# A hybrid decoder step on one core: chunk products regrouped by kind, part of the scaling moved to ScalarE, two weight splits moved

## What is computed

```python
xc, dtc, bc, cc = r(x), r(dt), r(bm), r(cm)          # r: split in chunks
acs = jnp.cumsum(dtc * a, axis=2)
decay = jnp.exp(jnp.where(causal, seg, -jnp.inf))     # seg: differences of acs
scores = jnp.einsum('bclgn,bcsgn->bclsg', cc, bc)
wgt = scores[..., None] * decay * dtc[:, :, None]
y_diag = jnp.einsum('bclsgk,bcsgkp->bclgkp', wgt, xc)
decay_end = jnp.exp(acs[:, :, -1:] - acs) * dtc
states = jnp.einsum('bclgn,bclgk,bclgkp->bcgkpn', bc, decay_end, xc)
# h is carried from chunk to chunk:  h * chunk_decay + state
y_off = jnp.einsum('bclgn,bcgkpn,bclgk->bclgkp', cc, h_prev, jnp.exp(acs))
y = y_diag + y_off;  y = y + xs * d_skip
```

## Time and profile before

| | us |
|---|---|
| median of 3 runs (lowest to highest) | 2364.67 (2363.91 to 2365.6) |
| the profiled execution | 2363.87 |
| its span, first to last instruction | 2362.2 |
| TensorE busy | 2325.2 (98%) |
| VectorE busy | 1218.1 (52%) |
| ScalarE busy | 593.6 (25%) |
| mean granted TensorE clock | 0.996 |

### The profile page before, as it was taken

The page is one execution under the profiler, slowest core; times in us unless marked ns, Lnnn a source line. Parts: engine busy times, 40 slices in busy tenths (PEclk is TensorE's granted clock), DMA queues, the critical chain, the costliest instruction groups (busy, mean ns, idle before and its releaser), DMA issues.

```text
span 2362.2 us, 37288 instructions
## 1 busy us (share of the span) xinstructions
PE 2325.2 (98%) x15084; PEld 2248.2 (95%) x15084; DVE 1218.1 (52%) x2337; ACT 593.6 (25%) x1020; POOL 58.4 (2%) x100
## 2 busy tenths in 40 slices
PE   8999999999999999999999999999999999999999
PEld 7999999999999999985799988999999999999998
DVE  6544444444445775465867435256444444444445
ACT  6111111111112332235623134141111111111112
POOL 0000000000000000022300000000000000000000
PEclk9999999999999999998999999999999999999999
DMA  4111111111111421057524324311111111111111
GB/s 148 42 48 36 53 36 53 53 49 39 36 53 41 127 58 37 28 171 226 173 81 127 125 97 152 111 54 36 54 36 53 53 52 36 36 52 43 46 36 74
DMA packets 185422, 169.23 MB, mean 72 GB/s; under 512 B 6660, under 2 KB 165138, under 8 KB 185066
## 3 DMA queue, kind: packets, MB, share of 16 engines
q1 hardware_dynamic: 185329, 167.94, 22.9%
HBM read 147.98 MB, written 20.04 MB: 71 GB/s over the span
## 4 chain that ended last, share of the span: by engine, by line
PE 61%; DVE 2%; ACT 1%; issue 0%; DMA 0%; DVEq 0%; ACTq 0%
PE bank L2265 17%; PE bank L2266 17%; PE bank L2267 17%; PE bank L2857 1%; PE bank L2869 1%; PE bank L2753 1%; PE bank L2757 1%; PE bank L2961 1%; PE bank L2889 1%; PE bank L2762 0%; PE bank L2878 0%; DMA w_raw<-in_w_mem_v_dram 0%; PE bank L2911 0%; PE bank L2773 0%; PE bank L2697 0%
## 5 line engine op out<-in xcount | busy, mean ns | idle before, releaser
L2265 PE MATMUL bank<-h_hi,w_hi 128*128 128x352 f32 x3120 | 1011.2, 324 | 5.8 <-DVE h_lo L1351 2.8
L2266 PE MATMUL bank<-h_lo,w_hi 128*128 128x352 f32 x3120 | 1000.6, 321 | 0.0
L2267 PE MATMUL bank<-h_hi,w_lo 128*128 128x352 f32 x3120 | 1000.3, 321 | 0.0
L2265 PEld LDWEIGHTS bank<-h_hi,w_hi 128*128 128x128 f32 x3120 | 586.2, 188 | 7.9 <-DVE w_lo L1322 3.2
L2266 PEld LDWEIGHTS bank<-h_lo,w_hi 128*128 128x128 f32 x3120 | 587.3, 188 | 0.0
L2267 PEld LDWEIGHTS bank<-h_hi,w_lo 128*128 128x128 f32 x3120 | 585.7, 188 | 0.0
L1416 DVE SCALAR_TENSOR_TENSOR x<-bank,x 128x352 f32<-128x352 f32 x528 | 276.3, 524 | 187.6 <-PE bank L2267 187.3
L2265 PE MATMUL bank<-mid_hi,w_hi 128*128 128x352 f32 x1056 | 341.3, 323 | 1.2 <-DVE x L1416 1.2
L2266 PE MATMUL bank<-mid_lo,w_hi 128*128 128x352 f32 x1056 | 338.4, 320 | 0.0
L2267 PE MATMUL bank<-mid_hi,w_lo 128*128 128x352 f32 x1056 | 338.1, 320 | 0.0
L1322 DVE TENSOR_TENSOR w_lo<-w_raw,w_hi 128x1024 fp32r<-128x1024 f32 x190 | 229.0, 1233 | 52.3 <-ACT w_hi L862 50.4
(11 more groups left out here) (333 smaller groups left out, 1465.3 us busy)
## 6 DMA issues: line engine op xcount, KB each, us to landing
w_raw<-in_w_gate_dram SPq DMA_DIRECT2D x44, 512.0 KB, 3.9
w_raw<-in_w_up_dram SPq DMA_DIRECT2D x44, 512.0 KB, 4.7
w_raw<-in_w_down_dram SPq DMA_DIRECT2D x44, 512.0 KB, 4.2
w_raw<-in_w_in_dram SPq DMA_DIRECT2D x18, 512.0 KB, 4.7
x_spill<-x SPq DMA_DIRECT2D x6, 1408.0 KB, 6.2
kring<-in_cache_mem_k_dram SPq DMA_DIRECT2D x8, 1024.0 KB, 5.0
vring<-in_cache_mem_v_dram SPq DMA_DIRECT2D x8, 1024.0 KB, 5.0
dec<-acs_row SPq DMA_DIRECT2D x8, 768.0 KB, 5.9
```

Of the source, the lines that this page charges most:

```text
L2265: eng.matmul(out, a_hi, b_hi, start=first, stop=False)
L2266: eng.matmul(out, a_hi, b_lo, start=False, stop=False)
L2267: return eng.matmul(out, a_lo, b_hi, start=False, stop=last)
```

## The change

Four edits, all of the chunk stage. (1) In `chunk_y` the 12 skip products come first, then the 12 of dec by xdt, then the 12 of hT by cea; before, the three kinds alternated for every pair of heads. (2) From chunk 3 on, heads 8 to 11 of xdt are made by ScalarE, four `activation` instructions with a scale from dt_, in a new `take_x` of ScalarE; VectorE's `take_x` ends after L1803. A new semaphore `xa_ready` is waited for by GpSimd ahead of xde and by TensorE ahead of chunk_y. (3) In ScalarE's loop the order for chunks 3 to 8 is `take_x`, `take_b`, `decays`; before it was `decays`, `take_b`. (4) The two `w_split` after steps 2 and 4 become one `w_pair` in step 8, ahead of `gate_chunk`, and SyncE issues the two next w_out tiles after the two reloads of x.

```diff
@@ SyncE
-                if q_ == 6:
-                    for k in (4, 5):
-                        unit(U_OUT + k, wv["w_out"][:, :, k * P:(k + 1) * P])
             for n in range(2):
                 eng.wait_ge(c_sum, (4, 7)[n])
                 eng.dma_start(x[:, 0:YT, cols(n)], x_spill[:, 0:YT, cols(n)]).then_inc(s_back[n], 16)
+            for k in (4, 5):
+                unit(U_OUT + k, wv["w_out"][:, :, k * P:(k + 1) * P])
@@ GpSimd, end_weight
+                if q_ > 2:
+                    eng.wait_ge(xa_ready, q_ - 2)
@@ ScalarE
+            def take_x(q_):
+
+                o = q_ % 2
+                eng.wait_ge(t1, 2 * q_ + 2)
+                eng.wait_ge(yd_ready, q_ - 1)
+                eng.wait_ge(xe_ready, q_ - 2)
+                for h in range(8, HEADS):
+                    ins = eng.activation(xdt[o][:, h, :], bank[1][:, HD * (h - 8):HD * (h - 7)], ACT.Copy,
+                                         scale=dt_[:, q_ - 1, h:h + 1])
+                ins.then_inc(xa_ready, 1)
...
             for q_ in range(1, CH + 1):
-                if q_ < CH:
+                if q_ == 1:
+                    decays(2)
+                    take_b(2)
+                elif q_ < CH:
+                    take_x(q_ + 1)
+                    take_b(q_ + 1)
                     decays(q_ + 1)
-                    take_b(q_ + 1)
@@ VectorE, take_x and the loop
-                eng.wait_ge(t1, 2 * q_ + 2)
-                link(eng.tensor_tensor(xdt[o][:, 8:12, :], bank[1][:, 0:256].rearrange("p (h d) -> p h d", d=HD), by_dt(8, 12),
-                                       ALU.mult))
+                if q_ < 3:
+                    eng.wait_ge(t1, 2 * q_ + 2)
+                    link(eng.tensor_tensor(xdt[o][:, 8:12, :], bank[1][:, 0:256].rearrange("p (h d) -> p h d", d=HD),
+                                           by_dt(8, 12), ALU.mult))
                 eng.sem_inc(xd_ready, 1)
...
+                if q_ == CH:
+                    w_pair(U_OUT + 2)
                 gate_chunk(q_)
...
-                if q_ in (2, 4):
-                    w_split(U_OUT + q_ // 2 + 1)
@@ TensorE, chunk_y
+                wait(eng, xa_ready, q_ - 2)
                 wait(eng, h_upd, q_ - 1)
...
+                outs, ends = [], (6, 7, 10, 11)
+                for h in range(HEADS):
+                    j, half = h // 2, slice(64 * (h % 2), 64 * (h % 2) + 64)
+                    outs.append(a[half, P * j:P * j + P] if j < 4 else b[half, P * (j - 4):P * (j - 4) + P])
+                    eng.matmul(outs[h], dsk[half, j, :], xs[half, j, tok], start=j in (0, 4), stop=False)
+                for h in range(HEADS):
+                    if h % HG == 0:
+                        eng.wait_ge(wg_ready, 2 * q_ + h // HG + 1)
+                    mm = eng.matmul(outs[h], xdt[q_ % 2][:, h, :], dec[(q_ - 1) % 3][:, h, :], start=False,
+                                    stop=q_ == 1 and h in ends)
+                if q_ > 1:
+                    for h in range(HEADS):
+                        if h % HG == 0:
+                            eng.wait_ge(c_ready, 2 * (q_ - 2) + h // HG + 1)
+                        mm = eng.matmul(outs[h], hT[:, HD * h:HD * h + HD], cea[q_ % 2][:, h, :], start=False, stop=h in ends)
                 mm.then_inc(yd_ready, 1)
```

More of the change, by code:

```diff
@@ L326, in build @@
                                                  sem("s_decd"))
+        xa_ready = sem("xa_ready")
         t1, t1_ev, ud_ready, seg_ready, e_done, sc_ready, sm_done = (
```

## The result

| | before | changed |
|---|---|---|
| median of ten runs each | 2364.62 us | 2379.01 us |
| the profiled execution | 2363.87 | 2378.53 |
| its span | 2362.2 | 2376.8 |
| mean granted TensorE clock | 0.996 | 0.992 |

The ratio is 1.0062, with a 95% interval of 1.0051 to 1.0072: the changed kernel is slower by 14.4 us. The forecast was 2379.3.

A forecast was written before the change was run, and what follows sets the result against it. It took TensorE to hold the middle steps, VectorE about one microsecond behind. The new chain through ScalarE gave +12.5 us, the clock +2.1: +14.6, profiled 2378.5, median 2379.3 us; range 2374 to 2389.

The forecast's parts named there:

- The ring: Chunk steps: decays queue behind the wait on `xd_ready`, making VectorE's step a serial chain through ScalarE, 12.02 us against 9.87.
- The sum: Chunk stage up to the last gate: +12.5 us from longer periods and shorter products, +2.1 for the clock, +14.6 us.
- The clock: TensorE idle 3.6 us before each chunk_y; slow starts covered in chunks 3 to 7, costing 0 to 4.25, +2.1, in chunk 8.
- Rival (b): TensorE's clock never falls, since other small products lie in the gap: 12.5 us alone, 2377.2; 20%.
- rival (e): Nothing measurable, because ScalarE's chain overlaps in a way not seen; 5%.
- rival (c): TensorE's clock stays low over most of the steps, and chunk 8 costs its whole 4.25: +24, 2389; 18%.
- The grouping: chunk_y: 10 fewer shape changes at 0.15 us each, products from 5.75 to 4.25 us; 1.8 off in chunk 1.
- rival (d): Grouping doesn't shorten chunk_y's products, only chunks 1 and 8 lose: +2.2, 2381.5; counted within the forecast's 52%.
- The first paragraph: Kernel before, middle steps: TensorE, busy all 9.87 us of step 4, holds them, with VectorE about one microsecond behind.
- rival (a): Faster: decays still ready when VectorE asks, step 8.45 us; -11 us, 2353.5; 5%.
- The terms at nothing: Scaled copies (1.2 to 1.8 us), moved `w_split` (3.9 at most) and w_out loads cost nothing; loads 0, bounds 0 and +1.

The follow-up runs named there:

- Order only: Kernel before with ScalarE's order alone changed, btok copied ahead of the decays for chunks 3 to 8; 2383.15 us, ratio 1.0076.
- square ahead: Changed kernel with ScalarE's `y_square` moved between the btok copy and the decays, from chunk 3 on; 2383.58 us, ratio 1.0082.
- filled gap: Changed kernel with 14 small unused products added on TensorE ahead of chunk 8's products; 2374.94 us, ratio 1.0046.
- Grouping only: Kernel before with the grouped products of `chunk_y` alone, without the wait for `xa_ready`; 2361.95 us, ratio 0.9989.
- decays first: Changed kernel with ScalarE's old order put back, decays ahead of the scaled copies and btok; 2359.29 us, ratio 0.9978.
- late xde: "decays first" kernel plus a GpSimd wait for VectorE's gate ahead of the next chunk's xde; 2352.39 us, ratio 0.9951.

## Why the prediction was right, point by point

**The ring.** It runs as worked out. Step by step, predicted and measured: L1820 to btok copy 0.79 and 0.78; to the first Relu 0.28 and 0.28; two halves of Relu and the Exp between 1.89 + 0.75 + 1.89 and 1.88 + 0.75 + 1.88; the second Exp until `weigh` 0.84 and 0.88; `weigh` to `scale_c` 1.01 and 0.87; `scale_c` to gate 1.74 and 1.74; 1.36 and 1.47 as before. The period is 11.89, not 12.02. The 1.01 was a distance in step 1, where 0.05 us of idle time lie between the two records; in the ring they overlap, and the distance is 0.87. "Order only" and "square ahead" confirm the cause by two edits of their own.

**The sum.** +14.6 was forecast for the last gate. It is measured at 1199.93 against 1185.27, +14.66, and that it is so close is luck. The term for the clock, 2.1 us, was the middle of bounds 0 and 4.25, with no row or run to place it; the runs showed 2.66 in its place, and errors cancel:

| | predicted | measured |
|---|---|---|
| gate 1 | 1118.62 | 1118.94 |
| L1820 (before L1803) of chunk 3 | 1121.45 | 1121.71 |
| five periods | 60.10 | 59.46 |
| update_state of step 7 | 1192.10 | 1191.59 |
| chunk 8's products | 4.25 + 2.1 | 6.88 |
| last gate, later by | 14.6 | 14.66 |

The update of step 7 came 0.5 us earlier than said and the lower clock cost 0.56 us more (6.88 - 4.22 = 2.66 against 2.1). Gate 1 did not stay: `scale_c` waited 0.29 us for the load of cea, which nothing in the sum had.

**The clock.** Forecast: low for part of chunk 8, covered in the middle. Both held. All of chunk 8's first two kinds ran at a granted clock of 0.50 (2.82 and 2.83 us instead of 1.53), and "filled gap" gave back 3.0 us at the last gate, 2.64 of them behind the start of chunk 8's products. I had "TensorE idle about 3.6 us before each chunk_y"; recorded are 2.21, 4.12, 1.82, 3.44, 1.81, 3.44 and 3.24. In the middle the next stretch after a slow chunk is short, since the products took longer, and the one after it is long again. Ahead of chunk 8 it is long, 3.24 us, although chunk 7 was slow: step 7 has no transposes and no scores for a later chunk to make, which my 3.6 us for every step left out. That would explain why a slow start fell on chunk 8, where nothing covers it; no run tests it. Rival (b), no fall of the clock, is out by the 0.50 of chunk 8; rival (e), nothing measurable, by the ratio's interval; rival (c) was right that the clock would fall in half of the middle steps, and wrong that this would cost: the gate waits for TensorE once.

**The grouping.** 4.25 forecast and 4.22 to 4.23 measured where the granted clock is 1.00, against 5.72 before: 1.5 us for 10 changes of shape fewer, so my estimate of 0.15 us each holds, and rival (d) is out. In chunk 1, at a granted clock of 0.50 in both, the products take 5.51 us after 7.48, 2.0 off where I had 1.8.

**The first paragraph was wrong.** It let TensorE hold the middle steps, from its 9.87 busy out of 9.87 us. "Grouping only" takes 1.5 us of TensorE's out of most steps and leaves the first four periods unchanged, at 8.9 and 10.06. VectorE held them; TensorE had no gap because it was falling behind VectorE's pace, and only the last periods and the last gate felt it. That did not touch the forecast, which lives on the ring, but it did spoil rival (a): its -11 us supposed a step of 8.45. Without the ring the real kernel gained 4.6 us, because the step is VectorE's, `weigh` stands behind GpSimd, and chunk 8's first kind of products ran at a granted clock of 0.50 ("decays first"). 2353.5 was the time of a kernel with late xde, not of this one.

**The terms at nothing.** The four scaled copies took 0.93 us together, under the lower bound of 1.2, and ended at 1142.7, 3.5 us before the btok copy. The w_out loads cost 0: no wait for them shows up to 1300 us of the span. `w_pair` was to take 3.9 us at most; it took 4.48. VectorE's and GpSimd's timelines of the changed kernel:

```profile
1104.04 2.35 DVE L1339 TENSOR_TENSOR w_lo<-w_raw,w_hi 128x1024 fp32r<-128x1024 f32 x2
...
1192.88 4.48 DVE L1339 TENSOR_TENSOR w_lo<-w_raw,w_hi 128x1024 fp32r<-128x1024 f32 x2
...
1199.93 0.69 DVE L1854 TENSOR_TENSOR xs<-bank,z 128x512 f32<-128x512 f32 x1 [2.58 <-PE bank L2781]
```

```profile
1192.87 1.47 POOL L822 TENSOR_TENSOR hc<-hT,cd 128x768 f32<-128x768 f32 x1 [8.99 <-DVEq L1869]
...
1194.30 1.98 POOL L814 TENSOR_TENSOR z<-z 128x384 f32<-128x384 f32 x1
1196.36 1.32 POOL L815 TENSOR_TENSOR z<-z 128x128 f32<-128x128 f32 x1
1197.75 0.46 POOL L816 TENSOR_TENSOR z<-z 128x128 f32<-128x128 f32 x1
```

The same two instructions take 2.35 us where GpSimd is idle. The bound doubled one `w_split` that met the last 0.9 us of one GpSimd instruction; here the two, 2.47 and 2.01 us long, run beside hc and the squares from start to end. It is still covered: 2.58 us of waiting for TensorE are left ahead of the last gate. Part of that cover was made by the clock: with chunk 8's products at 4.23 us, in "filled gap", the gate follows the pair without a wait.

## What to carry to other kernels

When a call is moved in an in-order queue, write down which wait stands in front of it in the new place and who waits for what is queued behind it; if that is the engine that gives the wait, add up the ring once round, from start times, and compare it with the step. An engine without a gap in a middle step need not hold the pace; it can be falling behind one that does, and then its shorter work comes back as a wait. Before work is taken off an engine, look whether its next instruction is held up by a neighbour: here one wait that moved a GpSimd instruction brought some 6 us, more than the 4.7 of the edits that helped. And before a shortening is added to the sum, look at the granted clock where it counts: of the 1.5 us that the grouping saves, chunk 8 kept 0.2 or less in three kernels, where the granted clock over its products was 0.71, 0.72 and 0.75.

## What the runs showed of the hardware

Some VectorE and GpSimd instructions took longer side by side here than alone. Two `weigh` instructions take 1.74 us alone, 2.50 or 2.91 by start times beside xde, and in both cases what follows them starts 1.60 us after its end. GpSimd's xde, which comes first there, keeps its 1.47 us. Beside `w_pair` the squares on GpSimd were longer too: the 128x384 one took 1.98 us against 1.00 in the kernel before, where VectorE stood idle, and a 128x128 one 1.32 us, against 0.46 for the next once `w_pair` was over. The update of hT, which reads hc and a bank, takes 0.69 us in every kernel, also in "late xde", where it starts at 1142.28 beside an xde of 1142.08 to 1143.55.

The granted clock differed from step to step within one kernel. In the changed kernel it was 1.00 over the first kind of products (1.53 us) after recorded idle stretches of 1.81, 1.82 and 2.21 us, and 0.50 to 0.58 (2.50 to 2.82 us) after those of 3.24 to 4.12. That TensorE is late once and early the next time makes the steps of the changed kernel differ in pairs on TensorE, while VectorE's are all alike.

The length of the idle stretch doesn't decide it alone. The clock was 1.00 over the first kind after 3.56 us ("grouping only", chunk 2) and 3.36 ("filled gap", chunk 2), and 0.52 after 1.34 ("square ahead", chunk 7), 0.50 after 1.61 ("grouping only", chunk 4) and 0.50 after 1.85 ("decays first", chunk 8). Nor is it the same in every execution: chunk 1's products, with the same work ahead of them, took 5.49 to 5.51 us in six of the kernels that group them, at a clock of 0.50 or 0.51, and 2.92 at 1.00 in "grouping only" and "filled gap". So the clock of one place in one execution is not yet a property of the kernel; that chunk 8 is slow in the changed one rests on one timeline and on the 3.6 us between the medians of "filled gap" and the changed kernel.
